# 32 tokens leave the first expert product of a two-layer block: their chosen rows are gathered and dotted on VectorE

## What is computed

```
def peer(xn, w_q, sub_keys, u_tab, v_tab):
    ...
    best, pos = lax.top_k(cand.reshape(n_tok, PEER_HEADS, kk), PEER_TOPK)
    idx = jnp.take_along_axis(cand_idx.reshape(n_tok, PEER_HEADS, kk), pos, axis=-1)
    g = jax.nn.softmax(best, axis=-1).astype(xn.dtype)
    def block(args):
        tb, ib, gb = args
        ue = u_tab[ib]
        act = jax.nn.gelu(jnp.einsum("phkd,pd->phk", ue, tb))
        ve = v_tab[ib]
        return jnp.einsum("phk,phkd->pd", gb * act, ve)
```

## Time and profile before

| | |
|---|---|
| median of 3 runs | 2202.69 us (2201.32 to 2202.81) |
| profiled execution | 2200.7 us |
| its span, first to last instruction | 2198.5 us |
| mean granted TensorE clock | 0.985 |
| busy: TensorE, VectorE, ScalarE, GpSimd | 95%, 76%, 37%, 35% of the span |
| choosing stage with the early tiles, about | 842 to 1085 us |
| spread rounds (96 tiles of 5.52 us), about | 1088 to 1620 us |
| late rounds (8 tiles of 5.06 us) | 1620 to 1660 us |
| second product | 1659 to 2185 us |

### The profile page before, as it was taken

The page is one execution under the profiler, slowest core; times in us unless marked ns, Lnnn a source line. Parts: engine busy times, 40 slices in busy tenths (PEclk is TensorE's granted clock), DMA queues, the critical chain, the costliest instruction groups (busy, mean ns, idle before and its releaser), DMA issues.

```text
span 2198.5 us, 35247 instructions
## 1 busy us (share of the span) xinstructions
PE 2095.4 (95%) x11175; PEld 1849.3 (84%) x11175; DVE 1677.9 (76%) x3276; ACT 819.0 (37%) x1343; POOL 769.9 (35%) x672
## 2 busy tenths in 40 slices
PE   6998988979999998999899999999999999999997
PEld 4886788758888877899899999999998888888886
DVE  3776655677778744999688888888867888888887
ACT  4444423422322224244433333333333333333333
POOL 2000044500000000334478888988742222222221
PEclk9999999989999999999999999999999999999999
DMA  6643100405234224124477988988789999999995
GB/s 136 90 63 39 20 1 23 131 14 138 69 95 112 79 78 162 58 84 141 166 252 257 318 290 285 318 283 299 253 302 343 334 340 336 338 337 339 336 336 200
DMA packets 229810, 428.45 MB, mean 195 GB/s; under 512 B 18500, under 2 KB 155876, under 8 KB 229476
## 3 DMA queue, kind: packets, MB, share of 16 engines
q1 hardware_dynamic: 173108, 255.96, 38.6%
q0 software_dynamic: 41472, 151.01, 19.8%
q10 hardware_dynamic: 15152, 20.51, 2.6%
HBM read 381.28 MB, written 46.14 MB: 194 GB/s over the span
## 4 chain that ended last, share of the span: by engine, by line
PE 49%; DMA 1%; DVE 0%; POOL 0%; issue 0%; ACT 0%; SPq 0%; DVEq 0%; POOLq 0%
PE bank L2222 23%; PE bank L2205 20%; PE bank L2186 4%; PE bank L2194 2%; DMA v_gg<-weights 0%; DMA acts<-u_weight_lo 0%; POOL row_slot L1957 0%; DVE u_spread L2379 0%; DVE v_residual L2369 0%; POOL u_two L2128 0%; DVEq L2051 0%; ACT u_spread L2469 0%; SPq L2066 0%; DVE u_two L2341 0%; ACT u_weight_lo L2433 0%
## 5 line engine op out<-in xcount | busy, mean ns | idle before, releaser
L2222 PE MATMUL bank<-u_hi,u_one 128*128 128x512 f32 x768 | 299.0, 389 | 2.9 <-DVE u_two L2341 2.9
L2222 PE MATMUL bank<-u_hi,u_two 128*128 128x512 f32 x768 | 298.8, 389 | 0.0
L2222 PE MATMUL bank<-u_lo,u_one 128*128 128x512 f32 x768 | 298.8, 389 | 0.0
L2205 PE MATMUL bank<-xt_hi,u_hi 128*128 128x384 f32 x832 | 287.1, 345 | 0.0
L2205 PE MATMUL bank<-xt_hi,u_lo 128*128 128x384 f32 x832 | 278.9, 335 | 0.0
L2205 PE MATMUL bank<-xt_lo,u_hi 128*128 128x384 f32 x832 | 278.6, 335 | 0.0
L1957 POOL DMA_INDIRECT row_slot<-in_peer_v_dram,row_index x128 | 139.4, 1089 | 390.8 <-DVE row_x L2349 368.1
L2414 ACT ACTIVATE u_hi<-xh 128x1024 fp32r<-128x1024 f32 x128 | 135.9, 1061 | 331.5 <-PE bank L2222 330.9
L2338 DVE TENSOR_TENSOR u_lo<-xh,u_hi 128x1024 fp32r<-128x1024 f32 x128 | 156.8, 1225 | 80.0 <-ACT u_hi L2414 79.9
L1641 POOL TENSOR_TENSOR k_wlo<-q_raw,k_whi 128x2048 fp32r<-128x2048 f32 x4 | 18.7, 4670 | 466.3 <-ACT k_whi L1769 466.3
L2128 POOL TENSOR_TENSOR u_two<-u_match,u_weight_hi 128x512 fp32r<-128x512 f32 x96 | 163.5, 1703 | 50.8 <-DVE u_match L2268 50.0
(11 more groups left out here) (440 smaller groups left out, 4915.1 us busy)
## 6 DMA issues: line engine op xcount, KB each, us to landing
xh<-in_peer_v_dram SPq DMA_DIRECT2D x128, 512.0 KB, 5.4
xh<-in_peer_u_dram SPq DMA_DIRECT2D x104, 512.0 KB, 4.8
x_raw<-in_w_in_dram SPq DMA_DIRECT2D x56, 512.0 KB, 6.8
v_ga<-acts SPq DMA_DIRECT2D x128, 192.0 KB, 5.4
acts<-xh ACTq DMA_DIRECT2D x102, 192.0 KB, 4.3
weights<-u_spread POOLq DMA_DIRECT2D x32, 512.0 KB
v_gg<-weights SPq DMA_DIRECT2D x128, 128.0 KB, 5.2
p_raw<-in_w_in_dram SPq DMA_DIRECT2D x12, 1024.0 KB, 10.3
```

The source lines that it names most:

```text
L2205: mm = pe.matmul(k.ps[4 + b][:, 0:DENSE], w[b][:, c, :], x[:, c, 0:DENSE], start=(c == 0 and w is uhi and x is hi), stop=(c == DC - 1 and ...
L2222: mm = pe.matmul(k.ps[q][:, :], h[b][:, t * P:(t + 1) * P], w[b][:, f], start=start and h is hhi and w is vhi, stop=stop and h is hlo, ski ...
```

## The change

The dense product of the first table now covers 352 tokens (`DOTTED`) in place of 384; each of its matmuls has 32 columns fewer, in the early tiles too. The 32 tokens between (`ROWED`) are treated like the last ones, at the cost of 32 more gathers: of each token the 128 chosen rows are spread over four lanes of 32 partitions, so that a gather of 128 rows brings 4 rows for each of the 32 tokens. Their tokens stand four times in a tile `row_xa`, their indices and weights in `row_index_a` and `row_weight_a`, which the choosing stage fills: one multiplication on GpSimd, four small DMAs on SyncE's queue and eight small operations on VectorE behind the copies of the choice.

- The spread rounds have 144 fetches and dots in place of 120: one, two, one, two in the four tiles of a round, both dots of a tile ahead of `keep`. The sixth slot is a free row of `xh`. In the first 16 rounds two of the six are of the 32 tokens, all later ones of the last 128. The late rounds have 16 dots in place of 8.
- The weights of the 32 tokens are multiplied by the GELU of their dots: at the start of the fifth chunk ScalarE waits for the 96th dot and takes the GELU, at the start of the sixth VectorE multiplies, transposes and splits (four small operations), and GpSimd's `weigh` of step 88 waits for that. The columns of these tokens in `acts` are set to 1, so the second product stays as it is, with 384 tokens.
- Six fetches, not five, stand ahead of the first `weigh`.
- The loads on SyncE are written out tile by tile in place of a loop; two tiles of the second product (`v_ga`) lie in `row_xa`, and its first loads wait for dots.
- The stores of the grids stay where they were.

```diff
-SLOTS = 5
+SLOTS = 6
+ROWED = 32
+DOTTED = DENSE - ROWED
+LANES = P // ROWED
...
@@ -1752,7 +1764,7 @@
                         pe.wait_ge(s["sc_kept"], after(4 * steps + 1 + e))
                     for c in range(DC):
                         for w, x in ((u_hi, hi), (u_hi, lo), (u_lo, hi)):
-                            mm = pe.matmul(k.ps[6 + e % 2][:, 0:DENSE], w[e % 4][:, c * P:(c + 1) * P], x[:, c, 0:DENSE],
+                            mm = pe.matmul(k.ps[6 + e % 2][:, 0:DOTTED], w[e % 4][:, c * P:(c + 1) * P], x[:, c, 0:DOTTED],
                                            start=(c == 0 and w is u_hi and x is hi), stop=(c == DC - 1 and w is u_lo))
...
@@ -1821,10 +1833,17 @@
                         act.wait_ge(early_out[e % 4], 16 * (e // 4))
                     if e == EARLY - 2:
                         act.wait_ge(s["reduced"], after(steps))
-                    act.activation(act_of(e), k.ps[6 + e % 2][:, 0:DENSE], ACT.Gelu_apprx_tanh).then_inc(u_made, 1)
+                    if e < 4 or e >= EARLY - 2:
+                        act.wait_ge(ones_made, after(1))
+                        act.activation(act_of(e)[:, DOTTED:DENSE], ones[:, :], ACT.Copy)
+                    act.activation(act_of(e)[:, 0:DOTTED], k.ps[6 + e % 2][:, 0:DOTTED], ACT.Gelu_apprx_tanh).then_inc(u_made, 1)
...
+                for lane in range(LANES):
+                    to, of_own = slice(lane * ROWED, (lane + 1) * ROWED), lambda n: (
+                        sel[own, n, lane, heads * (LAST - 1):heads * LAST, :].rearrange("p h a -> p (h a)"))
+                    dve.scalar_tensor_tensor(out=rows["index_a"][to, :], in0=of_own(0), scalar=float(NKEYS), in1=of_own(1),
+                                             op0=ALU.mult, op1=ALU.add).then_inc(rows_done, 1)
+                    dve.tensor_copy(rows["weight_a"][to, :], of_own(2)).then_inc(rows_done, 1)
+
...
+DOTS = P + ROWED
+BOTH = 16
+AT_TILE = ((0,), (1, 2), (3,), (4, 5))
+ROWED_AT = {2: 0, 5: 1}
+LAST_AT = {0: 0, 1: 1, 3: 2, 4: 3}
...
-    late_from = spread_rounds * SLOTS
+    late_from = BOTH * len(LAST_AT) + (spread_rounds - BOTH) * SLOTS
     late = (P - late_from) // (rounds - spread_rounds)
+    dots_done = spread_rounds * SLOTS
...
-                with sp.Fori(0, spread_rounds) as n:
-                    for u in range(PER):
-                        load(n, u + 2)
-                sp.dma_start(rest[:, :, :], residual).then_inc(res_in, 16)
-                with sp.Fori(spread_rounds, rounds - 1) as n:
-                    for u in range(PER):
-                        load(n, u + 2)
-                for u in range(PER - 2):
-                    load(rounds - 1, u + 2)
+                for i in range(tiles):
+                    if i + 2 < tiles:
+                        load(i // PER, i % PER + 2)
+                    if i == steps:
...
+                    if u == 2:
+                        sp.wait_ge(dot_done, after(BOTH * SLOTS))
                     load_weighting(0, u)
                 for u in range(PER):
-                    if u == 1:
+                    if u == 0:
+                        sp.wait_ge(dot_done, after(last_dot(SLOTS - 1)))
+                    elif u == 1:
                         for b in range(2):
...
                     pool.wait_ge(match_done, after(step + 1))
+                    if step == DOTTED // TOK_TILE:
+                        pool.wait_ge(weight_split, after(5))
                     if step >= 2:
...
-                def fetch(n):
-                    if n >= P:
+                def fetch(g):
+                    if g >= DOTS:
                         return
-                    if n >= SLOTS:
-                        pool.wait_ge(dot_done, after(n - SLOTS + 1))
-                    fetch_row(pool, u_rows, rows, n, n % SLOTS, row_in)
+                    if g >= SLOTS:
+                        pool.wait_ge(dot_done, after(g - SLOTS + 1))
+                    at = g % SLOTS
+                    if g >= BOTH * SLOTS or at in LAST_AT:
+                        fetch_row(pool, u_rows, rows, last_rank(g), at, row_in)
+                    else:
+                        n = g // SLOTS * len(ROWED_AT) + ROWED_AT[at]
+                        fetch_at(pool, u_rows, rows["index_a"][:, n:n + 1], rows["slots"][at], row_in[at])
...
                         pool.wait_ge(spread_kept, after(CHUNK_STEPS * (c + 1)))
                     pool.dma_start(weights[at:at + NKEYS // PIECES, :, c * CHUNK:(c + 1) * CHUNK].rearrange("n p t -> p n t"),
-                                   spread[:, at:at + NKEYS // PIECES, slot:slot + CHUNK]).then_inc(piece_out[c % 2], 16)
-
-                for n in range(SLOTS):
-                    fetch(n)
+                                 spread[:, at:at + NKEYS // PIECES, slot:slot + CHUNK]).then_inc(piece_out[c % 2], 16)
+
...
-                    for _ in range((2 if u == PER - 1 else 1) if i < steps else (late // 2 if u % 2 == 0 else 0)):
+                    for _ in range(len(AT_TILE[u]) if i < steps else (late // 2 if u % 2 == 0 else 0)):
                         fetch(fetched)
                         fetched += 1
...
-                            mm = pe.matmul(k.ps[4 + b][:, 0:DENSE], w[b][:, c, :], x[:, c, 0:DENSE],
+                            mm = pe.matmul(k.ps[4 + b][:, 0:DOTTED], w[b][:, c, :], x[:, c, 0:DOTTED],
...
-                def dot(n, slot, count):
+                def dot(n, slot, count, x="x", to="dot"):
                     dve.wait_ge(row_in[slot], count * 16)
-                    dve.scalar_tensor_tensor(out=rows["slots"][slot][:, :], in0=rows["slots"][slot][:, :], scalar=1.0, in1=rows["x"][:, :],
-                                             op0=ALU.mult, op1=ALU.mult, accum_out=rows["dot"][:, bass.ds(n, 1)]).then_inc(dot_done, 1)
+                    dve.scalar_tensor_tensor(out=rows["slots"][slot], in0=rows["slots"][slot], scalar=1.0, in1=rows[x][:, :],
+                                             op0=ALU.mult, op1=ALU.mult, accum_out=rows[to][:, bass.ds(n, 1)]).then_inc(dot_done, 1)
+
+                def dots(n, c, u):
+                    for at in AT_TILE[u]:
+                        if c * chunk_rounds >= BOTH:
+                            dot(n * SLOTS + (at - BOTH * len(ROWED_AT)), at, n + 1)
+                        elif at in LAST_AT:
+                            dot(n * len(LAST_AT) + LAST_AT[at], at, n + 1)
+                        else:
+                            dot(n * len(ROWED_AT) + ROWED_AT[at], at, n + 1, "xa", "dot_a")
+
+                def rowed_weights(c):
+                    if c != CHUNKS - 1:
+                        return
+                    chain = Chain(dve, rowed_vec, done=1)
+                    dve.wait_ge(rowed_ready, after(1))
+                    chain(dve.tensor_tensor(rows["dot_a"][:, :], rows["dot_a"][:, :], rows["weight_a"][:, :], ALU.mult))
+                    chain(dve.transpose(chosen[:, 2, DOTTED:DENSE], rows["dot_a"][:, :]))
+                    dve.tensor_copy(weight_hi[:, DOTTED:DENSE], chosen[:, 2, DOTTED:DENSE]).then_inc(weight_split, 1)
+                    dve.wait_ge(weight_split, after(4))
+                    dve.tensor_tensor(weight_lo[:, DOTTED:DENSE], chosen[:, 2, DOTTED:DENSE], weight_hi[:, DOTTED:DENSE].bitcast(F32),
+                                      ALU.subtract).then_inc(weight_split, 1)
                 def body(n, c):
                     for u in range(PER):
...
-                            dot(n * SLOTS + u, u, n + 1)
+                            dots(n, c, u)
                             keep(c, step)
-                    dot(n * SLOTS + PER, PER, n + 1)
                 def late_rounds(n):
+                    if n == spread_rounds:
+                        dve.wait_ge(two_done, after(2 * steps))
+                        dve.wait_ge(match_done, after(steps + 1))
+                        for b in range(2):
...
@@ -2308,9 +2389,13 @@
                 dve.wait_ge(weight_split, after(3))
                 low(0, 0)
                 onehots(slice(0, TOK_TILE), 0)
-                loop(dve, body, late_rounds=late_rounds)
-
-                dve.wait_ge(dot_done, after(P))
+                for n in range(2, 4):
+                    dve.wait_ge(early_out[n], 16 * (EARLY // 4))
+                for b in range(2):
+                    dve.memset(ga[b][:, DOTTED:DENSE], 1.0).then_inc(ones_set, 1)
+                loop(dve, body, rowed_weights, late_rounds)
+
+                dve.wait_ge(dot_done, after(DOTS))
...
+                    if c * chunk_rounds == BOTH:
+                        act.wait_ge(dot_done, after(BOTH * SLOTS))
+                        act.activation(rows["dot_a"][:, :], rows["dot_a"][:, :], ACT.Gelu_apprx_tanh).then_inc(rowed_ready, 1)
                 high(0, 0)
-                for n in range(2, 4):
-                    act.wait_ge(early_out[n], 16 * (EARLY // 4))
+                act.wait_ge(ones_set, after(2))
                 loop(act, body, chunk)
```

65 lines of the change are left out of this document (47 added, 18 removed).

## The result

The changed kernel takes 2215.34 us (median of 4 runs, 2214.5 to 2217.25), the kernel before 2202.01 (4 runs, 2201.24 to 2202.81): a ratio of 1.0065, 95% interval 1.0051 to 1.0078. The forecast was 2213, slower. Its direction and its mechanism held. That its size came so close is partly luck: two small terms had the wrong sign, and other errors took back a part.

What follows compares the result with a forecast made beforehand. GpSimd and VectorE, taking turns, would replace TensorE as the bound in spread rounds: +22.6 - 3.4 - 6.1 - 2.5 - 2.5 + 1.25 + 1 = +10.3 us on 2200.7, so 2211.0, forecast 2213 against the median; range 2183 to 2240.

Steps and rivals of the forecast that it cites:

- What bounds the kernel: Spread rounds and second product: TensorE alone, 22.08 us a round; GpSimd and VectorE near, store runs 23.1 on GpSimd.
- Part 1: First product, 32 columns fewer: 0.318 us less a tile, TensorE's pace 5.20 us a tile, 20.8 a round.
- Part 2: Early tiles: TensorE transposes the choice up to 2.2 us earlier; with 0.3 for the last tile, -2.5 us.
- The bound of 0: Early tiles' smallest gain: nothing, if GpSimd's new multiplication holds up VectorE at the stage's start; other end -3.5 us.
- Part 3: Eight store rounds with six fetches: tiles of 6.7 and 5.75 us, 24.9 a round, +22.6 us before GpSimd's lead.
- The lead: GpSimd enters store runs ahead of TensorE: 3.4 us taken off the store rounds' cost once, none rebuilt.
- Part 4: Sixteen rounds without stores: VectorE's work plus waits for weighings make 21.7 us a round, -6.1 us.
- Part 5: The rest: one more fetch before the first weighing +1.25 us, late rounds -2.5, chunk starts +1, SyncE's waits nothing.
- the list of signs: Trace signs of right or wrong; wrong included a granted clock below 1.00 in spread rounds and dots waiting for rows.
- TensorE staying the bound: Rival, all rounds: GpSimd's blocked time falls into idle time and its lead carries it through stores; 2169 us, chance 0.06.
- stores alone binding: Rival: rounds between stores run at 20.8 us and rebuild the 3.4 us lead each time; 2183 us, chance 0.17.
- Every dot blocks in full: Rival, every round: blocked engine's work follows each dot; 27.6 us with stores, 22.6 without; 2249 us, chance 0.10.

Runs made afterwards that it cites:

- The last run: Changed kernel with stores respaced on SyncE, second dot behind the grid addition, residual load split, late dots redealt, choices turned after the last early tile: 2172.73 us.

## Why the prediction was right, and where it was not

**What bounds the kernel:** right. The reading that decided was that from store to store in the earlier trace rows, 5.53 us for one fetch and 6.55 for two, which the busy shares don't show, since GpSimd's lead covered it. From the thirteenth tile on, TensorE's spreading starts within 0.4 us of the end of GpSimd's weighing, and GpSimd's wait for one-hots fell from 47.2 us to 14.3 in the spread rounds.

**Part 1:** right. Matmuls of 352 columns stand 158 ns apart (24 in 3.80 us), forecast 160.5. A tile at TensorE's pace is 5.155 us (5.20), a late one 4.68 (4.74).

**Part 2:** wrong in sign, -2.5 forecast, +1.45 measured. The step that failed is "VectorE's chain of selections ends when it did". The bound of 0 named GpSimd's new multiplication; that did hold up one of VectorE's (3.43 us against 1.22), but the stage's first search began no later (879.15 against 879.37 us). The loss came from instructions that the change does not touch: GpSimd's subtractions for the early tiles follow TensorE's pace, and shifted against VectorE. TensorE's own gain became the 4.29 us wait.

**Part 3:** right. Tiles of 6.70 to 6.78 and 5.63 to 5.71 against 6.7 and 5.75; eight rounds cost +21.35 in place of +22.6. As assumed, the fetch gets in as the first dot ends and the second dot runs beside it (1237.76 us, 1.22 us long); the weighing behind pays 0.13 us where 0.2 was assumed. The run without the lane fetches shows the cause.

**The lead and Part 4:** right only together. The other fifteen rounds and the last three tiles gave 10.25 us, or 11.85 without what the two late chunks' starts add; forecast were 6.1 and 3.4. Rounds take 21.4 and not 21.7: the second dot of a tile loses 0.8 us to the weighings, where a full microsecond and some hops were allowed for. VectorE's two dots of such a tile and GpSimd's two weighings, in order of time:

```profile
1281.10 1.21 DVE L2335 SCALAR_TENSOR_TENSOR row_slot<-row_slot,row_x 128x1024 f32<-128x1024 f32 x1
...
1281.26 1.95 POOL L2180 TENSOR_TENSOR u_two<-u_match,u_weight_hi 128x512 fp32r<-128x512 f32 x1 [0.43 <-DVE u_match L2324]
...
1282.24 2.05 DVE L2335 SCALAR_TENSOR_TENSOR row_slot<-row_slot,row_xa 128x1024 f32<-128x1024 f32 x1
...
1283.17 2.02 POOL L2180 TENSOR_TENSOR u_two<-u_match,u_weight_lo 128x512 fp32r<-128x512 f32 x1
```

GpSimd's lead over the spreading was 2.34 us at the second tile, not 3.4, and it was used up ahead of the first store (0.17 us at the thirteenth tile): it bought two rounds of 20.6, about 1.5 us. The lead was costed too high and the gain of the other rounds too low, by a little more.

**Part 5:** the sixth fetch +1.5 up to the first spreading (forecast 1.25), the two chunk starts +1.6 (1). Behind the longer wait for that fetch, the lower clock made the first round 1.55 us longer than the next two; no term held it, and the list of signs named it as one of being wrong. The late tiles were mis-signed, -2.5 against +4.53. The step counted VectorE's work in that stage, 20 us in 38, and no bytes: it costed 16 rows as dots and not as 8 MB on DMA engines at 0.82. The list of what would be wrong named the sign, dots that wait for rows (2.21 us at 1642.73), without a price. SyncE's waits for dots, put at nothing, are 2.0 us in the changed kernel, where VectorE is later still, and 3.6 us with the residual moved, where the load that they hold back ends the wait.

**The rivals.** TensorE staying the bound and stores alone binding fall with the rounds of 21.4 and 24.7. "Every dot blocks in full" falls too: a store round would have been 27.6 us. The Trainium skill, page "SBUF — State Buffer", section "SBUF: two separate sides", has the later engine wait out the earlier one's hold. The trace agrees for a fetch (1.96 us when it starts 0.12 us into a dot) and for a weighing beside a dot (1.95). How often it costs anything is read from the trace alone: the fetch at 1232.23 us and three of the four weighings of that stretch pay nothing, and the fourth 0.13 us, since VectorE then waits for GpSimd or works from a bank. So blocked time was not added in full to the bound here; it fell first into the idle time of the engine that was not late.

The sum was +10.3 us for the profiled executions and they differ by 16.5; the medians differ by 13.3. The two wrong signs are 11 us, more than the whole forecast difference, of which the spread rounds gave back 2.8 and the second product 1.6. That the forecast of 2213 lies 2.3 us from the median is therefore partly luck; the larger terms of Parts 3 and 4 are not.

## What to carry to other kernels

Cost a moved product in the queue it goes to, at its worst stretch and with the gaps: 2.48 us of fetches a round, on a GpSimd without idle time in its store rounds, weighed more than the 1.3 us a round saved on TensorE. Count bytes as well as instructions wherever rows are gathered beside other loads, and ask of each queue what stands behind a large transfer. When one bound is taken away, look for the next in the same trace before expecting the gain: stores off GpSimd gave 25 us, and the order of the dots gave none by itself. The last run gave 17 us more, with five changes at once, so what each of them is worth is not shown.
